# Two norms at the seam of two blocks computed from one pass: one shared factor, and the meta tokens normed in the first layer

## What is computed

```python
def first_block(x, ...):
    for l in range(DEPTH):
        x = x + 0.5 * swiglu(rms_norm(x, ffn1_norm[l]), ...)
        x = x + mixer(rms_norm(x, mix_norm[l])) @ w_out[l]
        x = x + 0.5 * swiglu(rms_norm(x, ffn2_norm[l]), ...)
    return rms_norm(x, final_norm)              # norm A

def second_block(x, meta_tokens, norm_w, w_in, ...):
    h_res = jnp.concatenate([meta, x], axis=1)
    h = _rmsnorm(h_res, norm_w[l])              # norm B
    proj = h @ w_in[l]
    ...
    h_res = h_res + jnp.concatenate([y_mla, y_na], axis=-1) @ w_out[l]
    return h_res[:, N_META:]
```

## Time and profile before

| | |
|---|---|
| median of 3 runs | 1233.51 us (1232.77 to 1234.11) |
| the profiled execution, its own time | 1232.0 us |
| its span | 1230.2 us |
| PE busy | 1188.6 us (97% of the span) |
| DVE, ACT, POOL busy | 815.4, 656.6, 165.7 us |

### The profile page before, as it was taken

The page is one execution under the profiler, slowest core; times in us unless marked ns, Lnnn a source line. Parts: engine busy times, 40 slices in busy tenths (PEclk is TensorE's granted clock), DMA queues, the critical chain, the costliest instruction groups (busy, mean ns, idle before and its releaser), DMA issues.

```text
span 1230.2 us, 27307 instructions
## 1 busy us (share of the span) xinstructions
PE 1188.6 (97%) x10002; PEld 1147.1 (93%) x10002; DVE 815.4 (66%) x1390; ACT 656.6 (53%) x1121; POOL 165.7 (13%) x228
## 2 busy tenths in 40 slices
PE   6999999999999999999999999999998989998998
PEld 6999999799999999999999899999997887998888
DVE  6767664877777665777665877777656666555764
ACT  5555543656555544555544645555545666656652
POOL 3000000351000000000000450000000000401960
PEclk9999999999999999999999999999997999999999
DMA  7655754445566744556744446556642440544542
GB/s 280 207 190 191 252 169 136 139 155 190 190 200 204 233 160 139 189 200 205 235 162 137 138 155 198 195 188 223 216 158 69 137 131 8 172 155 136 174 154 87
DMA packets 56742, 210.91 MB, mean 171 GB/s; under 512 B 7200, under 2 KB 9280, under 8 KB 56544
## 3 DMA queue, kind: packets, MB, share of 16 engines
q1 hardware_dynamic: 54048, 203.45, 50.1%
q0 software_dynamic: 2480, 6.48, 1.8%
q10 hardware_dynamic: 144, 0.06, 0.0%
HBM read 208.91 MB, written 1.05 MB: 171 GB/s over the span
## 4 chain that ended last, share of the span: by engine, by line
PE 84%; DVE 7%; ACT 3%; issue 3%; POOL 2%; DMA 0%; DVEq 0%; ACTq 0%; SPq 0%
PE bank L1173 25%; PE bank L1174 25%; PE bank L1175 25%; DVE w_lo L748 3%; PE bank L1211 2%; PE bank L1521 2%; PE bank L1501 1%; DVE h_lo L767 1%; ACT w_hi L457 1%; PE bank L1486 1%; DVE probs L886 1%; PE bank L1423 1%; PE bank L1425 1%; PE bank L1424 1%; PE bank L1481 1%
## 5 line engine op out<-in xcount | busy, mean ns | idle before, releaser
L1173 PE MATMUL bank<-h_hi,w_hi 128*128 128x256 f32 (+1 forms) x1992 | 563.4, 283 | 16.9 <-DVE w_lo L748 11.7
L1174 PE MATMUL bank<-h_lo,w_hi 128*128 128x256 f32 (+1 forms) x1992 | 554.3, 278 | 0.0
L1175 PE MATMUL bank<-h_hi,w_lo 128*128 128x256 f32 (+1 forms) x1992 | 554.2, 278 | 0.0
L748 DVE TENSOR_TENSOR w_lo<-w_raw,w_hi 128x1024 fp32r<-128x1024 f32 (+1 forms) x360 | 466.9, 1301 | 73.5 <-ACT w_hi L457 73.2
L457 ACT ACTIVATE w_hi<-w_raw 128x1024 fp32r<-128x1024 f32 (+1 forms) x360 | 397.4, 1108 | 74.4 <-PE bank L1175 56.3
L1173 PEld LDWEIGHTS bank<-h_hi,w_hi 128*128 128x128 f32 x1992 | 377.1, 189 | 24.0 <-issue 19.5
L1174 PEld LDWEIGHTS bank<-h_lo,w_hi 128*128 128x128 f32 x1992 | 377.1, 189 | 0.9
L1175 PEld LDWEIGHTS bank<-h_hi,w_lo 128*128 128x128 f32 x1992 | 376.8, 189 | 0.0
L1173 PE MATMUL bank<-g_hi,w_hi 128*128 128x256 f32 x832 | 230.8, 277 | 1.5 <-DVE g_lo L893 0.8
L1175 PE MATMUL bank<-g_hi,w_lo 128*128 128x256 f32 x832 | 230.0, 276 | 0.0
L1174 PE MATMUL bank<-g_lo,w_hi 128*128 128x256 f32 x832 | 230.0, 276 | 0.0
(11 more groups left out here) (152 smaller groups left out, 1158.6 us busy)
## 6 DMA issues: line engine op xcount, KB each, us to landing
w_raw<-in_w SPq DMA_DIRECT2D x296, 512.0 KB, 3.3
w_raw<-in_wd SPq DMA_DIRECT2D x64, 704.0 KB, 4.1
w_raw<-in_relbias POOLq DMA_DIRECT2D x64, 64.0 KB, 2.3
btab_sb<-in_btab POOLq DMA_DIRECT2D x1, 1536.0 KB, 9.5
x_res<-in_xT SPq DMA_DIRECT2D x2, 512.0 KB, 5.0
out_T<-x_res SPq DMA_DIRECT2D x8, 128.0 KB, 1.7
rope_sb<-in_rope POOLq DMA_DIRECT2D x1, 272.0 KB, 3.6
mats_sb<-in_mats POOLq DMA_DIRECT2D x1, 192.0 KB, 4.0
```

Of the source, the lines that this page charges most:

```text
L748: dve.tensor_tensor(wlo[:, slot, at:at + cols], raw[:, slot, 0:cols], whi[:, slot, at:at + cols].bitcast(F32), ALU.subtract).then_inc(lo_r ...
L1173: pe.matmul(o, h, xh, start=first, stop=False)
L1174: pe.matmul(o, h, xl, start=False, stop=False)
L1175: return pe.matmul(o, lo, xh, start=False, stop=last)
```

## The change

`final_sums` replaces the two sums of the seam. During the last down projection POOL also multiplies each square by `w6` = g6² + 1e-6 and adds these up in `wacc`; PE sums `wacc` and the last square times its weight into one bank (the merged factor) and `acc` and the last square into another (the factor of norm A alone). `final_norm` scales x by g6·g7 and the merged factor straight into `h32`. The in-place scaling of x by norm A (`final_x`) is moved into the MLA projections, one tile behind each of outputs 8 to 15. The meta tokens need norm B only. Their squares, sum, factor and scaling are moved into the mixer stage of the first layer (the 16-column sum on PE and its Ln and Exp on ACT are in the loop over layers, so they run in both), and only their split in high and low parts is at the seam.

```diff
+        g67, w6 = fin[:, 0:KT], fin[:, KT:2 * KT]
+        wacc, wsq, w6_last = s_all[:, 0:T], s_all[:, T:2 * T], pr_all[:, 0:P]
+        rs6 = rel_all[:, 0:T]
+        xm = x[:, :, T:TM]
+        msq, hm = (h32[:, i, 0:KT * META].rearrange("p (k c) -> p k c", k=KT) for i in (3, 2))
+        hm_hi, hm_lo = (a[:].rearrange("p (k c) -> p k c", k=KT)[:, :, T:TM] for a in (hhi, hlo))
...
-            def add_squares(q, n=T, tiles=range(KT - 1)):
-                for i, k in enumerate(tiles):
+            def add_squares(q, weighted=False):
+                for k in range(KT - 1):
                     pool.wait_ge(sq_done[k % 2], q * 4 + k // 2 + 1)
+                    if weighted:
+                        dst = wsq if k else wacc
+                        if k:
+                            pool.wait_ge(wsq_step, 2 * k - 1)
+                        pool.tensor_scalar(dst, sq[:, k % 2, 0:T], w6[:, k:k + 1], None, ALU.mult).then_inc(wsq_step, 1)
                     if k == 0:
-                        pool.tensor_copy(acc[:, 0:n], sq[:, 0, 0:n]).then_inc(acc_step, 1)
+                        pool.tensor_copy(acc[:, 0:T], sq[:, 0, 0:T]).then_inc(acc_step, 1)
                     else:
-                        pool.wait_ge(acc_step, q * 7 + i)
-                        pool.tensor_tensor(acc[:, 0:n], acc[:, 0:n], sq[:, k % 2, 0:n], ALU.add)\
+                        pool.wait_ge(acc_step, q * 7 + k)
+                        pool.tensor_tensor(acc[:, 0:T], acc[:, 0:T], sq[:, k % 2, 0:T], ALU.add)\
                             .then_inc(acc_step, 1)
+                    if weighted and k:
+                        pool.wait_ge(wsq_step, 2 * k)
+                        pool.tensor_tensor(wacc, wacc, wsq, ALU.add).then_inc(wsq_step, 1)
+
+            def final_gains():
+                pool.tensor_tensor(g67, sml[:, 6 * KT:7 * KT], sml[:, 7 * KT:8 * KT], ALU.mult)
+                pool.tensor_tensor(w6, sml[:, 6 * KT:7 * KT], sml[:, 6 * KT:7 * KT], ALU.mult).then_inc(fin_set, 1)
+                pool.wait_ge(fin_set, 1)
+                pool.tensor_scalar(w6, w6, EPS, None, ALU.add).then_inc(fin_set, 1)
+                pool.wait_ge(fin_set, 2)
+
+            def meta_squares():
+                pool.wait_ge(c_loaded, C_LOADS)
+                pool.tensor_tensor(msq, xm, xm, ALU.mult).then_inc(msq_step, 1)
+                for n, w in enumerate((4, 2, 1)):
+                    pool.wait_ge(msq_step, n + 1)
+                    pool.tensor_tensor(msq[:, 0:w], msq[:, 0:w], msq[:, w:2 * w], ALU.add).then_inc(msq_step, 1)
+
+            def meta_normed():
+                pool.wait_ge(ms_done, 1)
+                pool.tensor_tensor(hm, xm, rs[:, 0, T:TM].unsqueeze(1).broadcast_to([P, KT, META]), ALU.mult)\
+                    .then_inc(hm_step, 1)
+                pool.wait_ge(hm_step, 1)
+                pool.tensor_tensor(hm, hm, sml[:, 7 * KT:8 * KT].unsqueeze(2).broadcast_to([P, KT, META]), ALU.mult)\
+                    .then_inc(hm_step, 1)
 
...
+            final_gains()
             for l in range(LAYERS):
                 add_squares(3 * l + 1)
+                if l == 0:
+                    meta_squares()
...
+                if l == 0:
+                    meta_normed()
                 add_squares(3 * l + 2)
-                add_squares(3 * l + 3)
-            add_squares(7, TM, range(0, KT, 2))
+                if l == LAYERS - 1:
+                    pool.tensor_copy(w6_last, w6[:, KT - 1:KT].broadcast_to([P, P])).then_inc(w6_set, 1)
+                add_squares(3 * l + 3, l == LAYERS - 1)
...
-            def norm(q, n=T):
-
-                act.wait_ge(sum_done, q + 1)
-                rstd(bank[SUM][:, 0:n], 0, D, n, q + 1)
+            def final_norm():
+
+                act.wait_ge(hm_step, 2)
+                act.activation(hm_hi, hm, ACT.Copy).then_inc(hm_hi_done, 1)
+                act.wait_ge(wsum_done, 1)
+                act.activation(lnv[:, 0, 0:T], bank[SUM][:, 0:T], ACT.Ln, scale=1.0 / D, bias=EPS * EPS)\
+                   .then_inc(ln_done, 1)
+                act.wait_ge(ln_done, 7)
+                act.activation(rs[:, 0, 0:T], lnv[:, 0, 0:T], ACT.Exp, scale=-0.5).then_inc(rstd_done, 1)
                 for k in range(KT):
-                    act.wait_ge(h32_done, q * KT + k + 1)
-                    act.activation(hhi[:, k * HS:k * HS + n], h32[:, k % 4, 0:n], ACT.Copy).then_inc(h_hi, 1)
+                    high(7, k, k % 4)
+                act.wait_ge(xsum_done, 1)
+                act.activation(lnv[:, 0, 0:T], bank[XSUM][:, 0:T], ACT.Ln, scale=1.0 / D, bias=EPS)\
+                   .then_inc(ln_done, 1)
+                act.wait_ge(ln_done, 8)
+                act.activation(rs6, lnv[:, 0, 0:T], ACT.Exp, scale=-0.5).then_inc(rstd_done, 1)
...
                         act.wait_ge(vt_done, l + 1)
+                        act.activation(lnv[:, 0, T:TM], bank[OUT][:, T:TM], ACT.Ln, scale=1.0 / D, bias=EPS)\
+                           .then_inc(ms_ln, 1)
                         act.activation(v32[:].rearrange("p t c -> p (t c)"), bank[OUT][:, 0:T], ACT.Copy)\
                            .then_inc(v_done, 1)
+                        act.wait_ge(ms_ln, l + 1)
+                        act.activation(rs[:, 0, T:TM], lnv[:, 0, T:TM], ACT.Exp, scale=-0.5).then_inc(ms_done, 1)
...
-            act.wait_ge(sum_done, 7)
-            rstd(bank[SUM][:, 0:T], 0, D, T, 7)
-            act.wait_ge(c_loaded, C_LOADS)
-            for k in range(KT):
-                act.wait_ge(fx_done, k + 1)
-                if k >= 2:
-                    act.wait_ge(sq_used[1] if k % 2 else acc_step, k // 2 if k % 2 else 7 * 7 + k // 2)
-                square(k % 2, x[:, k, :])
-            norm(7, TM)
+            final_norm()
...
-            def norm(q, n=T):
-                dve.wait_ge(rstd_done, q + 1)
+            def final_norm():
+                dve.wait_ge(hm_hi_done, 1)
+                dve.tensor_tensor(hm_lo, hm, hm_hi.bitcast(F32), ALU.subtract).then_inc(hm_lo_done, 1)
+                dve.wait_ge(h_lo, 7 * KT)
+                dve.wait_ge(rstd_done, 7)
                 for k in range(KT + 1):
                     if k < KT:
-                        dve.scalar_tensor_tensor(out=h32[:, k % 4, 0:n], in0=x[:, k, 0:n],
-                                                 scalar=sml[:, bass.ds(q * KT + k, 1)], in1=rs[:, 0, 0:n],
-                                                 op0=ALU.mult, op1=ALU.mult).then_inc(h32_done, 1)
+                        dve.scalar_tensor_tensor(out=h32[:, k % 4, 0:T], in0=x[:, k, 0:T], scalar=g67[:, k:k + 1],
+                                                 in1=rs[:, 0, 0:T], op0=ALU.mult, op1=ALU.mult).then_inc(h32_done, 1)
                     if k > 0:
-                        dve.wait_ge(h_hi, q * KT + k)
-                        c = (k - 1) * HS
-                        dve.tensor_tensor(hlo[:, c:c + n], h32[:, (k - 1) % 4, 0:n], hhi[:, c:c + n].bitcast(F32),
-                                          ALU.subtract).then_inc(h_lo, 1)
+                        low(7, k - 1, (k - 1) % 4)
+
+            def final_x(k):
+                if k == 0:
+                    dve.wait_ge(rstd_done, 8)
+                dve.scalar_tensor_tensor(out=x[:, k, 0:T], in0=x[:, k, 0:T], scalar=sml[:, 6 * KT + k:6 * KT + k + 1],
+                                         in1=rs6, op0=ALU.mult, op1=ALU.mult).then_inc(fx_done, 1)
...
-            dve.wait_ge(rstd_done, 7)
-            for k in range(KT):
-                dve.scalar_tensor_tensor(out=x[:, k, 0:T], in0=x[:, k, 0:T], scalar=sml[:, 6 * KT + k:6 * KT + k + 1],
-                                         in1=rs[:, 0, 0:T], op0=ALU.mult, op1=ALU.mult).then_inc(fx_done, 1)
-            dve.wait_ge(fx_done, KT)
             dve.wait_ge(c_loaded, C_LOADS)
             for kind, factor in (("qn", MLA_SCALE), ("qpe", MLA_SCALE), ("naq", HD ** -0.5)):
                 gain = G_HEAD + HEAD_GAIN[kind]
                 dve.tensor_scalar(sml[:, gain:gain + 1], sml[:, gain:gain + 1], factor, None, ALU.mult)
             dve.reduce_sum(vmask[:], ident[:, P - META:P], AX_X).then_inc(second_set, 1)
-            norm(7, TM)
+            final_norm()
...
+                    if outs is MLA and 8 <= n < 8 + KT:
+                        final_x(n - 8)
...
+            def final_sums():
+
+                pe.wait_ge(w6_set, 1)
+                pe.wait_ge(wsq_step, 2 * KT - 3)
+                pe.matmul(bank[SUM][:, 0:T], ones[:], wacc, start=True, stop=False)
+                pe.wait_ge(acc_step, 6 * 7 + KT - 1)
+                pe.matmul(bank[XSUM][:, 0:T], ones[:], acc[:, 0:T], start=True, stop=False)
+                pe.wait_ge(sq_done[1], 6 * 4 + 4)
+                pe.matmul(bank[SUM][:, 0:T], w6_last, sq[:, 1, 0:T], start=False, stop=True).then_inc(wsum_done, 1)
+                pe.matmul(bank[XSUM][:, 0:T], ones[:], sq[:, 1, 0:T], start=False, stop=True).then_inc(xsum_done, 1)
...
                     if i == 1:
+                        pe.wait_ge(msq_step, 4)
```

(36 more changed lines are left out.)

## The result

The changed kernel takes **1240.92 us** (median of 9 runs, 1236.69 to 1243.5), the kernel before 1233.51 (9 runs, 1232.25 to 1235.15). The ratio is 1.0057, 95% interval 1.0043 to 1.0071: 7.4 us slower, where 10.2 us less were forecast. The profiled execution took 1236.69 us. It is the fastest of the nine: its mean granted clock was 0.998, that of the median execution 0.996, so the profile shows less of the loss than the medians do.

The account below looks back on a forecast made before the run. PE, busy 97%, was taken as the bound, so only its lost time counts; 8.88 us (norm) plus 2.35 (clock) less 0.1 and 0.1 gave 11.0, or 9.5 with a short low stretch: 1223.3 us forecast, range 1221.3 to 1226.3.

Parts of the forecast that it names:

- The sum: Whole kernel: gains of 11.0, 9.5 or 8.7 us by clock case, giving 1222.5, 1224.0 or 1224.8; forecast 1223.3 us.
- What bounds the kernel now: PE is busy 97%, so only time it loses counts; at the seam no weight is multiplied for 13.08 us.
- What else is added: Mixer and MLA additions hide in waits, cost 0; uncovered, up to 2.4 us in the mixer, 3.9 in MLA.
- The second norm on the path: Seam: scaling into the operand buffer starts 8.88 us earlier, first product at 924.08; 0.1 us taken off.
- The clock: Kv products behind the seam: 0.8 to 2.4 us gained, depending on whether a 1.9 us pause brings a low stretch.
- POOL's weighted sum: Last down projection: 2.4 us a tile against 7.2 available, ending near 916, 4 us before PE asks; cost 0.
- stand in DVE's way: Rival, last down projection: 13 added POOL instructions hold DVE up in full, 11 us, time 1234; chance 0.03.
- the late weighted sum: Rival for "slower", at the seam: POOL's weighted sum comes after the last square, up to 1239.4 us; chance 0.02.
- the scalings of x: Rival, MLA stage: DVE's added scalings show, costing up to 3.9 us, time 1227.2; chance 0.07.
- the late weights: Rival, projections behind the seam: weights can't follow PE's 9 us earlier start, gain given back, 1230 to 1233; chance 0.04.
- What the new profile would show: Seam scaling 2.6 us after the residual add, product 1.6 later; POOL done 4 us early; DVE's head waits near 1.5.
- those I gave for "wrong": Second block and seam: PE waiting for a weight split or more for DVE, or DVE held by the meta tokens' part.

Follow-up runs that it names:

- experiment 1: Changed kernel with the spacers ahead of g_hi and y_hi cut from 64 to 48 columns, restoring the addresses of before: 1223.32 us, ratio to before 0.992.
- 3: Changed kernel with only the spacer ahead of g_hi cut to 48 columns, y_hi and y_lo left where the change put them: 1226.68 us, ratio 0.9957.
- 10: Changed kernel with both spacers cut to 48 columns, and DVE's scalings of x in one piece at the seam: 1225.23 us, ratio 0.9932.
- experiment 11: Changed kernel with both spacers cut to 48 columns, and three more POOL adds for each of seven last down-projection tiles: 1224.44 us, ratio 0.993.
- experiment 9: Changed kernel with both spacers cut to 48 columns, and four unused PE sums filling the pause at the seam: 1222.26 us, ratio 0.9915.
- experiment 8: Kernel before with 16 columns between g_hi and g_lo, so that g_lo alone moves, to the weights' position: 1247.62 us (one run).
- experiment 2: Kernel before with an unused 16-column tensor allocated where the change puts its gains, no instruction different: 1247.14 us, ratio 1.0115.

## Why the prediction was wrong, step by step

**The step that failed is "The sum": it has no term for PE's own rate.** It takes the gain of the rewritten places from 1232.0 and lets every other stage stand. It has no term for a product that itself gets slower: the step "What bounds the kernel now" reads PE's 97% as a bound that only pauses can worsen ("only time that PE loses counts"). "What else is added" counts instructions and forgets the tensor they write to. The missing term is +17.6 us (14.2 for g, 3.4 for y), measured as after less experiment 1; -10.2 + 17.6 = +7.4, the result. That this closes to the tenth is luck: with each kernel against its own kernel before it is a gain of 9.2 and a loss of 16.6. The row that would have asked the question is the spacer in the code, `g_hi_phase`, whose only purpose is an address.

**The second norm on the path: right.** Residual add to scaling 2.68 us (2.6 forecast), scaling to first product 1.54 (1.6). PE's two more sums lay ahead of the last square's, as said.

**The clock: right in kind.** Windows of the seam after, with the columns of the earlier trace rows:

```profile
935.85:937.30 1.45, 1.45 (x12) 1.45 (x13) 1.45 (x5) 0.83 (x2) 0.00 (x0) 1.00 0.00 0
937.30:940.70 3.40, 3.40 (x18) 3.40 (x17) 3.22 (x9) 2.13 (x6) 0.00 (x0) 0.50 0.00 0
940.70:942.50 1.80, 1.80 (x16) 1.80 (x16) 0.52 (x1) 1.18 (x2) 0.00 (x0) 1.00 0.03 9
```

One stretch of 3.40 us at 0.50 (the 1.2 GHz level) has 18 products under way, of which 15 start in it, 0.227 us apart; 14 were forecast for a short one, 23 stood in 5.26 us before. I had left open whether a pause of 2 us would bring such a stretch on. At the seam it did in the profiled executions of after and of experiments 1, 3, 10 and 11, each with a pause of 2.10 us, and in that of experiment 9, without the pause, it didn't. Elsewhere a pause of the same length leaves the clock alone. After has one ahead of a gate product, and the window behind it, of PE alone, has the full clock:

```profile
473.71 0.38 PE L1229 MATMUL bank<-h_hi,w_hi 128*128 128x256 f32 x1 [2.10 <-DVE h_lo L821]
```

```profile
473.71:477.12 3.41, 3.41 (x26) 1.00 0.05 12
```

So the pause is needed for the low stretch at the seam, as far as these six traces tell, but the length of a pause alone doesn't decide.

**POOL's weighted sum: 0, right,** though each tile takes more than the 2.4 us of the sum. The timeline of POOL after, behind the last residual add of its kind:

```profile
924.69 0.92 POOL L393 TENSOR_SCALAR scores_sb<-squares,final_gains 128x256 f32<-128x256 f32 x1 [5.30 <-ACT squares L518]
925.58 0.74 POOL L398 TENSOR_TENSOR ln_mean<-ln_mean,squares 128x256 f32<-128x256 f32 x1
926.27 1.72 POOL L402 TENSOR_TENSOR scores_sb<-scores_sb 128x256 f32<-128x256 f32 x1
```

The last add took 1.72 us, not 0.74; one of DVE's splits runs beside it, from 926.09 to 927.39. It ends at 928.0, and PE's first sum starts near 931.5: 3.5 us of slack, 4 forecast.

**What else is added: right that it costs nothing.** The mixer's additions can't be seen: after and experiment 1 both carry them, and the latter ends where the forecast without them does. In the MLA projections DVE's waits from 962 to 980 went from 5.4 us to 3.4:

```profile
DVE k_heads L1122 <- ACT rstd L523: 3.4, 5, 1.0
```

1.5 were forecast. PE's own waits there stay at 0.8 us.

**The rivals.** None was the true one. POOL does stand in DVE's way, but by 0.28 us a split and not in full, and experiment 11 shows that even twice the work costs PE nothing; the late weighted sum falls by the 3.5 us of slack, the scalings of x by 1 and 10, the late weights by 1 (same transfers, 1223.32). The rival for "slower" named 1239.4, near the result, by a mechanism that had no part in it.

**What the new profile would show.** The signs I listed came true or nearly so, and none of those I gave for "wrong". The list looked only where the diff is. The Trainium skill (SBUF — State Buffer, Who interferes with whom) says that a DVE instruction with two SBUF inputs contends with a GpSimd one that reads SBUF. The traces agree: the splits of DVE took 1.90 and 2.03 us beside POOL's added work, in place of 1.63. DVE had 9 us of idle time in experiment 11 to hide it, and the 64 bytes are a matter of PE's operands.

## What to carry to other kernels

A new tensor moves all that is allocated behind it, and here 64 bytes cost more than a whole norm gained: allocate it last, or take it from a spacer, and compare the addresses of PE's operands before and after any diff. When a kernel gets slower, count the products that start in a window of a stage that the change does not touch, first of all; a busy share of 100% and a clock of 1.00 say nothing of the rate. A prediction for a kernel that one engine bounds needs a term for that engine's rate, with the question what could change it.

## What the runs showed of the hardware

In the gate, up and down projections the rate of fp32 products of 256 columns depends on where the moving operand lies relative to the weights within 256 bytes: one every 0.113 us with it 64 bytes ahead, 0.117 to 0.120 us at the six other arrangements of the table, at the same granted clock. At the 2.4 GHz level that is some 272 and, at equal position, 288 cycles a product (an estimate from 7.47/66 and 7.91/66 us). A shift of 256 bytes changes nothing. It isn't the only thing that counts. In the mixer's output projection of before, with `g_hi` and `g_lo` at the good position as well, products of PE's timeline that lie 15 apart are 1.76 us apart, 0.117 each:

```profile
275.29 0.28 PE L1173 MATMUL bank<-g_hi,w_hi 128*128 128x256 f32 x1
...
277.05 0.28 PE L1173 MATMUL bank<-g_hi,w_hi 128*128 128x256 f32 x1
```

What slows them there I didn't find. Which memory structure causes the effect of the addresses stays open: products and weight loads run at the same time, but no view shows their accesses, and I didn't vary the two in steps small enough, nor one kind of operand at a time except in experiment 8. That the loss of experiment 2 is 2 to 3 us less than that of after stays open as well.

The fastest of these kernels is the changed one with its addresses back, 1223.32 us, or 1222.26 with PE's pause filled, which the runs can't tell apart. Both are 0.8% faster than before and 1.4 to 1.5% faster than after (1223.32/1240.92 = 0.986).
